# Chaining the second and third sums of a squared-relu group in PSUM, and adding every product into its output quadrants

## The chip, the cores and the metric

The kernel runs on one core of one Trainium2 chip. The metric is the device time of one execution in microseconds; the time shown is the median of several runs. All matrix products are float32r products made of three matmuls: each operand is cut into a high and a low part, and high x high, low x high and high x low are summed in PSUM.

## The reference

Two transformer-like blocks of width 1024 over 512 tokens. The first has two layers; each layer ends with a squared-relu MLP, and these two MLPs are what the change touches:

```python
def sq_relu_mlp(h, w_up, w_down):          # 1024 -> 4096 -> 1024
    return jnp.square(jax.nn.relu(h @ w_up)) @ w_down

# in first_block, for each of the two layers
h = rms_norm(x, ln_mlp_pre[i])
f = sq_relu_mlp(h, mlp_w_up[i], mlp_w_down[i])
x = x + rms_norm(f, ln_mlp_post[i]).astype(x.dtype)
```

The rest (a gated linear attention and a windowed attention before these MLPs, a second block with convolution, dilated attention and a gated MLP behind them) stays as it is.

## The kernel before, in words

The 4096 hidden columns of a layer are done in four parts of 1024. For the first three, the down projection is a seven-product (Strassen-like) scheme instead of eight products: a group "seven{layer}{o}" with o = 0 to 2, six groups in the kernel. The last part goes through the plain path (`t_ends`).

A group multiplies the hidden columns (AH, AL: high and low parts of seven combinations of the activations, made while the up products run) by seven combinations of four weight quadrants b11, b12, b21, b22. Each of the seven products ("b11", "b21", "t1", "b22", "t2", "t3", "t4") has two halves h = 0 and 1, so a group is 14 units. A unit is one weight tile of 128 x 1024 and 12 matmuls of 512 columns. The list STREAM gives their order: b11, b21, t1 (first halves), then their second halves, b22, t2, t3, t4. A product fills two PSUM banks (one per half of the 256 tokens that a combination has), by the table SEVEN_BANKS.

The weight tile of a unit comes into a raw slot (four of them, WR) by a DMA that SyncE issues. For t1 and t3, GpSimd then adds a second quadrant into the same slot with an accumulating DMA; for t2 and t4 it adds a further quadrant into the slot of t1, once the tile in it has been cut for t1 or t2. The order of GpSimd's issues is M_SUMS (`g_seven`). ScalarE makes the high part WH (`a_high`, L1299) and VectorE the low part WL (`v_low`, L2030), for which there are four slots; a slot is free when the unit four places earlier is done. Both engines run their programs in order: in step j of a group each first cuts unit j + 3 (`a_cut`, `v_cut`) and then does its other work. TensorE takes the units in order (`t_seven`): it waits for WL of the unit and, at the first half of a product, until the two banks are free.

VectorE empties the two banks of a product in one instruction of 128 x 1024 (`part`, L2448 in the first group of a layer, L2451 in the others), in the step after the product's second half: into four quadrants of MT and three buffers of PX, one accumulator for each product. Behind the third group, while the up products of the last part run, seven SBUF additions (`together`, L2460) make the four output quadrants from the seven accumulators. The last four weight tiles of the down projection may be cut when the seventh of these is done, since they lie over PX.

Of the kernel before, what the change touches and what calls it, by code (L numbers as in the profile page):

```python
# [144 lines left out]

def stream_of(name):

    return {"sevenf2": LAST_STREAM, "sevenv0": V_STREAM, "sevenw0": V_STREAM, "seveny0": Y_STREAM}.get(name, STREAM)


def plan(m, d):
# [70 lines left out]
    for layer in range(2):  # L222
        up, down = each(f"up{layer}", 32), each(f"down{layer}", 8)
        for o in range(3):
            add(f"up{layer}{o}", up[8 * o:8 * o + 8])
            seven(f"seven{layer}{o}", d[f"quart{layer}"][o].rearrange("j h p f -> h j p f"))
        add(f"up{layer}3", up[24:])
        add(f"down{layer}3", down, extra=m.EXTRA["mlp"], freed=("sum7", layer, 6))
        if layer == 0:
            add("swa_in", each("swa_in", 10))  # L230
            add("swa_out", each("swa_out", 8), extra=m.EXTRA["swa"], freed=("pv", "w", 15))
# [29 lines left out]
def memory(nc):  # L261
# [38 lines left out]
    def arena(name, shape, kb, dt=F32):  # L300
        return over(name, shape, base + int(kb * KB), dt)
# [13 lines left out]

    m.AH = arena("AH", [128, 4, 7, 256], 0, F32R)
    m.AL = arena("AL", [128, 4, 7, 256], 28, F32R)
    m.PX = arena("PX", [128, 3, 2, 512], 59)
    m.H3H = arena("H3H", [128, DC, T], 0, F32R)
    m.H3L = arena("H3L", [128, DC, T], 16, F32R)  # L320
    m.RW = over("RW", [128, 2, 2, T], acc)
# [61 lines left out]
def quarter(m, i, j):  # L383

    return m.MT[:, 2 * i:2 * i + 2, 512 * j:512 * j + 512]


def partial(m, what):

    if what in ("b21", "t2", "t3"):  # L390
        return m.PX[:, ("b21", "t2", "t3").index(what)]
    return quarter(m, *{"b11": (0, 0), "b22": (0, 1), "t4": (1, 0), "t1": (1, 1)}[what])


def mixes(m, key):
# [41 lines left out]
class Taps:  # L437
# [14 lines left out]
    def take(self, n):  # L452
# [22 lines left out]
GLA_O = (6, 7)  # L475
STREAM = [("b11", 0), ("b21", 0), ("t1", 0), ("b11", 1), ("b21", 1), ("t1", 1), ("b22", 0), ("b22", 1), ("t2", 0), ("t2", 1),
          ("t3", 0), ("t3", 1), ("t4", 0), ("t4", 1)]
LAST_HIDDEN = (7, 15, FC2 - 1)
LAST_STREAM = [("b11", 0), ("b21", 0), ("t1", 0), ("b22", 0), ("b11", 1), ("b21", 1), ("t1", 1), ("t2", 0), ("t2", 1), ("b22", 1),
               ("t3", 0), ("t3", 1), ("t4", 0), ("t4", 1)]  # L480
SIDE = {"b11": 0, "b21": 1, "t4": 2, "t3": 3, "t1": 4, "t2": 5, "b22": 6}
SIDE_PART = {0: "a", 1: "b", 2: "b", 3: "s", 4: "s", 5: "s", 6: "s"}
M_SUMS = [("t1", 0), ("t1", 1), ("t2", 0), ("t2", 1), ("t3", 0), ("t3", 1), ("t4", 0), ("t4", 1)]
F_SUMS = [("t1", 0), ("t1", 1), ("t2", 0), ("t3", 0), ("t3", 1), ("t2", 1), ("t4", 0), ("t4", 1)]
LAST_BANKS = {"b11": 0, "b21": 2, "t1": 4, "b22": 6, "t2": 0, "t3": 0, "t4": 2}
LAST_PARTS = {"b11": (((0, 0), 1),), "b21": (((0, 0), 1),), "t1": (((0, 1), 1), ((1, 1), 1)), "b22": (((0, 1), 1),),
# [9 lines left out]
Y_BANKS = {"b11": 4, "b21": 6, "t1": 2, "t2": 4, "b22": 2, "t3": 4, "t4": 0}  # L496
V_DECAYS, V_TURNS = (1, 4, 7, 10), (3, 6, 9, 12)
SEVEN_BANKS = {"b11": 0, "b21": 2, "t1": 4, "b22": 6, "t2": 0, "t3": 2, "t4": 4}
FFN_PARTS = {"b11": (((0, 0), 1), ("u2", 1)), "b21": (((0, 0), 1),), "t1": (((0, 1), 1), ((1, 1), 1)), "b22": (((0, 1), 1),),
             "t2": (("u2", 1),), "t3": (((1, 0), 1), ((1, 1), -1)), "t4": (((1, 0), 1),)}  # L500
GLA_DS = ((2, 3), (4, 5))
# [443 lines left out]
def t_seven(e, k, key, o):  # L945

    m, name = k.m, f"seven{key}{o}"
    u, stream = k.at[name], stream_of(name)
    last = name == "sevenf2"

    def pairs(j, h, b, f, v, start, stop):

        x = k.units[u + j]
        n = x.n // 4
        for q in range(n):
            p, w = 2 * h + q, slice(512 * q, 512 * q + 512)
            xh, xl = m.AH[:, p, f, tile(v)], m.AL[:, p, f, tile(v)]
            e.wait_ge(*k.on("side", key, 4 * o + p, SIDE_PART[f]))
            e.matmul(m.ps[b + v], xh, x.wh[:, w], start=start and q == 0, stop=False, skip_group_check=last)  # L959
            e.matmul(m.ps[b + v], xl, x.wh[:, w], start=False, stop=False, skip_group_check=last)  # L960
            y = e.matmul(m.ps[b + v], xh, x.wl[:, w], start=False, stop=stop and q == n - 1, skip_group_check=last)  # L961
        return y

    for j, (what, h) in enumerate(stream):
        b, f = (LAST_BANKS if last else SEVEN_BANKS)[what], SIDE[what]
        e.wait_ge(*k.on("wlo", u + j))
        if last and what == "t4":
            if h == 0:
                continue
            for v in range(2):  # L970
                e.wait_ge(*k.on(*k.free[b + v]))
                pairs(j - 1, 0, b, f, v, True, False)
                y = pairs(j, 1, b, f, v, False, True)
                y.then_inc(*(k.mark("unit", u + j) if v else k.mark("front", what)))
            continue
        for v in range(2):
            if h == 0:
                e.wait_ge(*k.on(*k.free[b + v]))
            y = pairs(j, h, b, f, v, h == 0 and not (last and what in ("t2", "t3")), h == 1)
            if last and what == "t2" and h and v == 0:  # L980
                y.then_inc(*k.mark("front", what))
        y.then_inc(*k.mark("unit", u + j))
        if h == 1:
            for v in range(2):
                k.free[b + v] = ("part", key, o, what, v) if last and what == "t2" else ("part", key, o, what)
# [1440 lines left out]
def v_mlp(e, k, layer):  # L2426
    m, at = k.m, k.at
    post, then = ("post_mlp0", "mix1") if layer == 0 else ("post_mlp1", "in2")

    def others(p):  # L2430

        v_mix(e, k, layer, p, ("sqr", at[f"up{layer}{p // 4}"] + 2 * (p % 4) + 1))
        v_side_b(e, k, layer, p)

    def plain(i):

        p, c = i // 2, i % 2
        e.wait_ge(*k.on("hidh", at[f"up{layer}3"] + i - 24))
        e.tensor_tensor(m.H3L[:, i - 24, :], m.RW[:, p % 2, c, :], m.H3H[:, i - 24, :].bitcast(F32), A.subtract).then_inc(
            *k.mark("hid", layer, i - 24))  # L2440

    def part(o, what):

        u = at[f"seven{layer}{o}"] + STREAM.index((what, 1))
        src, acc = pair(m, SEVEN_BANKS[what]).rearrange("p (a f) -> p a f", a=2), partial(m, what)
        e.wait_ge(*k.on("unit", u))
        if o == 0:
            e.tensor_copy(acc, src).then_inc(*k.mark("part", layer, o, what))  # L2448
        else:
            e.wait_ge(*k.on("part", layer, o - 1, what))  # L2450
            e.tensor_tensor(acc, src, acc, A.add).then_inc(*k.mark("part", layer, o, what))  # L2451

    def together(n):

        c11, c12, c21, c22 = (quarter(m, i, j) for i in range(2) for j in range(2))
        p2, u2, u3 = (m.PX[:, i] for i in range(3))
        out, a, b, op = ((u2, c11, u2, A.add), (c11, c11, p2, A.add), (u3, u2, u3, A.add), (c21, c21, u3, A.add),
                         (c12, c12, c22, A.add), (c12, c12, u2, A.subtract), (c22, c22, u3, A.subtract))[n]
        e.wait_ge(*(k.on("sum7", layer, n - 1) if n else k.on("part", layer, 2, "t4")))
        e.tensor_tensor(out, a, b, op).then_inc(*k.mark("sum7", layer, n))  # L2460

    def ups(o):

        u = at[f"up{layer}{o}"]
        for j in range(8):
            v_cut(e, k, u + j + 3)
            if o == 3:
                if j:
                    plain(24 + j - 1)
                    together(j - 1)  # L2470
                continue
            if j % 2:
                v_side_a(e, k, layer, 4 * o + j // 2)
            if j > 1 and j % 2 == 0:
                others(4 * o + j // 2 - 1)
            if j > 2 and j % 2:
                v_side_s(e, k, layer, 4 * o + j // 2 - 1)

    def seven(o):

        u = at[f"seven{layer}{o}"]
        for j in range(14):
            v_cut(e, k, u + j + 3)
            if j == 0:
                others(4 * o + 3)
            if j == 1:
                v_side_s(e, k, layer, 4 * o + 3)
            if j and STREAM[j - 1][1]:
                part(o, STREAM[j - 1][0])
        part(o, STREAM[13][0])  # L2490

    for o in range(3):
        ups(o)
        seven(o)
    ups(3)
    v_cut(e, k, at[f"down{layer}3"] + 3)
    plain(31)
    v_ends(e, k, at[f"down{layer}3"], at["swa_in" if layer == 0 else "glu"], post, then)
# [513 lines left out]
def g_seven(e, k, key, o):  # L3012

    m, name = k.m, f"seven{key}{o}"
    u = k.at[name]
    for what in F_SUMS if key == "f" else M_SUMS:
        j = stream_of(name).index(what)
        x = k.units[u + j]
        e.wait_ge(*k.on(*x.sum_of))
        e.dma_start(raw(m, x.raw)[:, 0:128 * x.n], x.more, accum_op=A.add).then_inc(*k.mark(f"added{x.raw}", u + j, by=16))  # L3020
# [243 lines left out]
```

## Time and profile before

| | |
|---|---|
| runs | 1903.17 us median of 3 (1901.72, 1903.17, 1905.87) |
| span of the profiled execution | 1900.5 us; it has no other time of its own, and is 2.7 us below the median |
| TensorE (PE) busy | 1890.5 us, 99% |
| VectorE (DVE) busy | 1339.4 us, 70% |
| ScalarE (ACT) busy | 985.3 us, 52% |
| GpSimd (POOL) busy | 95.3 us, 5% |
| matmuls of the groups (L959 to L961) | 3 x 490, of which 6 x 168 in the two MLPs |
| DMA | 249.8 MB, mean 131 GB/s |

Matmuls are pipelined: one of 512 columns is shown with 0.39 us, and the next begins 0.23 us after it. The six groups begin at 270.4, 352.0, 433.6, 757.6, 839.2 and 920.8 us. Units are counted from 0 within a group.

### The profile page before, as it was taken

The numbers are of one execution on the slowest core, as the hardware profiler recorded it, in microseconds if no ns is written. First come the engines' busy times: TensorE is split into PE (matmuls) and PEld (weight loads), VectorE is DVE, ScalarE is ACT, GpSimd is POOL, SyncE is SP. The second block draws the span as 40 slices with busy tenths as digits, with TensorE's granted clock in tenths as the row PEclk, the third lists the DMA queues.
The fourth block names the chain that finished last, engine by engine and source line by source line (L and its number), as shares of the span: only waits on it lengthen the run. The fifth ranks groups of instructions, "written<-read, shape, count | busy, mean of one in ns | idle before, by whom it ended". The sixth has DMA issues, their size and how long they took to land. (4 is left out here: it accounts for less than half of the span.)

```text
span 1900.5 us, 25399 instructions
## 1 busy us (share of the span) xinstructions
PE 1890.5 (99%) x9486; PEld 1555.8 (82%) x9486; DVE 1339.4 (70%) x1988; ACT 985.3 (52%) x1587; POOL 95.3 (5%) x114
## 2 busy tenths in 40 slices
PE   9999999999999999999999999999999999999999
PEld 8877888887888778888888988667788888888887
DVE  7656665656566766665566788998897867767867
ACT  5634464544546746454444435788445446545454
POOL 0100000101000000000100000000000000100101
PEclk9999999999999999999999999999999999999999
DMA  7632156757323114756752356222224634644735
GB/s 230 155 100 94 73 142 180 166 162 202 123 79 144 46 56 132 201 139 173 180 162 67 112 143 167 89 90 78 89 91 143 166 89 155 155 148 118 199 95 122
DMA packets 69676, 249.79 MB, mean 131 GB/s; under 512 B 7730, under 2 KB 7986, under 8 KB 68916
## 3 DMA queue, kind: packets, MB, share of 16 engines
q1 hardware_dynamic: 55728, 198.88, 31.0%
q0 software_dynamic: 13824, 49.29, 14.8%
q8 instruction: 77, 1.26, 0.3%
q14 instruction: 43, 0.35, 0.1%
q10 hardware_dynamic: 4, 0.00, 0.0%
HBM read 246.05 MB, written 2.10 MB: 131 GB/s over the span
## 5 line engine op out<-in xcount | busy, mean ns | idle before, releaser
L545 PE MATMUL ps<-HH,WH 128*128 128x512 f32 (+1 forms) x1696 | 626.2, 369 | 0.9 <-ACT AT L1736 0.9
L547 PE MATMUL ps<-HH,WL 128*128 128x512 f32 (+1 forms) x1696 | 621.2, 366 | 0.0
L546 PE MATMUL ps<-HL,WH 128*128 128x512 f32 (+1 forms) x1696 | 620.9, 366 | 0.0
L1299 ACT ACTIVATE WH<-WR 128x1024 fp32r<-128x1024 f32 x333 | 348.9, 1056 | 479.8 <-PE ps L547 315.3
L2030 DVE TENSOR_TENSOR WL<-WR,WH 128x1024 fp32r<-128x1024 f32 (+1 forms) x332 | 403.1, 1218 | 263.1 <-ACT WH L1299 262.4
L545 PEld LDWEIGHTS ps<-HH,WH 128*128 128x128 f32 x1696 | 319.9, 189 | 62.5 <-issue 11.6
L547 PEld LDWEIGHTS ps<-HH,WL 128*128 128x128 f32 x1696 | 319.9, 189 | 52.2
L546 PEld LDWEIGHTS ps<-HL,WH 128*128 128x128 f32 x1696 | 320.0, 189 | 50.7
L959 PE MATMUL ps<-WH,AH 128*128 128x512 f32 x490 | 191.0, 390 | 0.4 <-DVE WL L2030 0.4
L960 PE MATMUL ps<-WH,AL 128*128 128x512 f32 x490 | 190.7, 389 | 0.0
L961 PE MATMUL ps<-WL,AH 128*128 128x512 f32 x490 | 190.6, 389 | 0.0
L2576 DVE SCALAR_TENSOR_TENSOR M<-AP,PAR,M 128x512 f32<-128x512 f32 x240 | 166.1, 753 | 0.1
L959 PEld LDWEIGHTS ps<-WH,AH 128*128 128x128 f32 x490 | 92.0, 188 | 20.8 <-DVE WL L2030 1.7
L961 PEld LDWEIGHTS ps<-WL,AH 128*128 128x128 f32 x490 | 92.0, 188 | 19.0
L960 PEld LDWEIGHTS ps<-WH,AL 128*128 128x128 f32 x490 | 92.0, 188 | 19.0
L1919 ACT ACTIVATE UP<-ps 128x512 f32<-128x512 f32 x44 | 26.4, 599 | 116.5 <-PE ps L547 116.5
L3020 POOL DMA_DIRECT2D WR<-in_quart x48 | 41.8, 988 | 818.5 <-DMA WR<-in_quart 751.2
L2881 DVE SCALAR_TENSOR_TENSOR RW<-UP,PAR,RW 128x512 f32<-128x512 f32 x44 | 33.1, 752 | 43.3 <-ACT RW L1925 42.5
L2881 DVE SCALAR_TENSOR_TENSOR M<-UP,PAR,M 128x512 f32<-128x512 f32 x44 | 33.1, 752 | 37.7 <-ACT M L1925 36.9
L1307 ACT ACTIVATE HL<-X 128x1024 fp32r<-128x1024 f32 x24 | 25.4, 1060 | 34.8 <-DVE X L2091 24.4
L1318 ACT ACTIVATE HH<-ps 128x512 fp32r<-128x512 f32 x48 | 26.1, 594 | 31.2 <-PE ps L598 31.0
L1527 ACT ACTIVATE RW<-RW 128x512 f32<-128x512 f32 x64 | 40.6, 634 | 2.0
(386 smaller groups left out, 2606.9 us busy)
## 6 DMA issues: line engine op xcount, KB each, us to landing
WR<-in_up SPq DMA_DIRECT2D x96, 512.0 KB, 4.2
WR<-in_quart SPq DMA_DIRECT2D x60, 512.0 KB, 3.6
WR<-in_quart POOLq DMA_DIRECT2D x48, 512.0 KB, 6.3
WR<-in_in SPq DMA_DIRECT2D x48, 512.0 KB, 3.6
WR<-in_down SPq DMA_DIRECT2D x16, 512.0 KB, 3.5
WR<-in_quartf SPq DMA_DIRECT2D x14, 512.0 KB, 3.5
WR<-in_quartf POOLq DMA_DIRECT2D x14, 512.0 KB, 5.6
MT<-in_up SPq DMA_DIRECT2D x12, 512.0 KB, 4.1
```

Of the source, the lines that this page charges most:

```text
L545: e.matmul(ps, wh, hi[:, c, cols], start=c == 0, stop=False)
L546: e.matmul(ps, wh, lo[:, c, cols], start=False, stop=False)
L547: y = e.matmul(ps, wl, hi[:, c, cols], start=False, stop=c == x.n - 1)
L959: e.matmul(m.ps[b + v], xh, x.wh[:, w], start=start and q == 0, stop=False, skip_group_check=last)
L960: e.matmul(m.ps[b + v], xl, x.wh[:, w], start=False, stop=False, skip_group_check=last)
L961: y = e.matmul(m.ps[b + v], xh, x.wl[:, w], start=False, stop=stop and q == n - 1, skip_group_check=last)
L1299: e.activation(x.wh[:, 0:n], raw(m, x.raw)[:, 0:n], AF.Copy).then_inc(*k.mark("whi", u))
L1527: e.activation(buf, buf, AF.Square).then_inc(*k.mark("sqr", u))
L2030: e.tensor_tensor(x.wl[:, 0:n], raw(m, x.raw)[:, 0:n], x.wh[:, 0:n].bitcast(F32), A.subtract).then_inc(*k.mark("wlo", u))
L2576: e.scalar_tensor_tensor(m.M[:, c, :], m.AP[:, c, t:t + T], par(m, "conv_w", c * 31 + t, 1), m.M[:, c, :], A.mult, A.add).then_inc(*k.mark ...
L2881: e.scalar_tensor_tensor(tmp, m.UP[:, 2 * (i % 2) + g, t:t + T], par(m, "fcw", (i + FC2 * g) * 3 + t, 1), tmp, A.mult, A.add).then_inc(*k. ...
L3020: e.dma_start(raw(m, x.raw)[:, 0:128 * x.n], x.more, accum_op=A.add).then_inc(*k.mark(f"added{x.raw}", u + j, by=16))
```

## The change

The t2 products are accumulated onto b11 in banks 0 and 1, and t3 onto t2 in the same banks: their first matmuls no longer start a new accumulation. t4 goes ahead of t3, in TensorE's stream and in GpSimd's additions, and takes banks 2 and 3. So t2's banks hold b11 + t2 and t3's hold b11 + t2 + t3 when VectorE reads them, and every product is added to or subtracted from its output quadrants at once: nine operations in a group in place of seven, four of them copies in the first group of a layer. PX and `together` are gone. The last weight tiles of the down projection are free when the third group's last unit is done. The loops of `v_mlp` and `a_mlp` that place a cut and an evacuation in a step stay as they are, with M_STREAM for STREAM.

```diff
 def stream_of(name):
 
+    if name[:6] in ("seven0", "seven1"):
+        return M_STREAM
...
-        add(f"down{layer}3", down, extra=m.EXTRA["mlp"], freed=("sum7", layer, 6))
+        add(f"down{layer}3", down, extra=m.EXTRA["mlp"], freed=("unit", at[f"seven{layer}2"] + 13))
...
-    m.PX = arena("PX", [128, 3, 2, 512], 59)
...
+M_STREAM = STREAM[:10] + STREAM[12:] + STREAM[10:12]
...
-M_SUMS = [("t1", 0), ("t1", 1), ("t2", 0), ("t2", 1), ("t3", 0), ("t3", 1), ("t4", 0), ("t4", 1)]
+M_SUMS = [("t1", 0), ("t1", 1), ("t2", 0), ("t2", 1), ("t4", 0), ("t4", 1), ("t3", 0), ("t3", 1)]
...
+M_BANKS = {"b11": 0, "b21": 2, "t1": 4, "b22": 6, "t2": 0, "t3": 0, "t4": 2}
+M_STARTS = ("b11", "b21", "t1", "b22", "t4")
+M_PARTS = {"b11": (((0, 0), 1),), "b21": (((0, 0), 1),), "t1": (((0, 1), 1), ((1, 1), 1)), "b22": (((0, 1), 1),),
+           "t2": (((0, 1), -1),), "t4": (((1, 0), 1),), "t3": (((1, 1), -1), ((1, 0), 1))}
...
     for j, (what, h) in enumerate(stream):
-        b, f = (LAST_BANKS if last else SEVEN_BANKS)[what], SIDE[what]
+        b, f = (LAST_BANKS if last else M_BANKS if chained else SEVEN_BANKS)[what], SIDE[what]
...
-            y = pairs(j, h, b, f, v, h == 0 and not (last and what in ("t2", "t3")), h == 1)
+            y = pairs(j, h, b, f, v, h == 0 and not (last and what in ("t2", "t3")) and not (chained and what not in M_STARTS), h == 1)
...
     def part(o, what):
 
-        u = at[f"seven{layer}{o}"] + STREAM.index((what, 1))
-        src, acc = pair(m, SEVEN_BANKS[what]).rearrange("p (a f) -> p a f", a=2), partial(m, what)
+        u = at[f"seven{layer}{o}"] + M_STREAM.index((what, 1))
+        src = pair(m, M_BANKS[what]).rearrange("p (a f) -> p a f", a=2)
         e.wait_ge(*k.on("unit", u))
-        if o == 0:
-            e.tensor_copy(acc, src).then_inc(*k.mark("part", layer, o, what))
-        else:
-            e.wait_ge(*k.on("part", layer, o - 1, what))
-            e.tensor_tensor(acc, src, acc, A.add).then_inc(*k.mark("part", layer, o, what))
...
+        for to, sign in M_PARTS[what]:
+            acc = quarter(m, *to)
+            if to not in prior:
+                e.wait_ge(*k.on("turned", f"mlp{layer}", 3, 1))
+                if sign > 0:
+                    e.tensor_copy(acc, src).then_inc(*k.mark("part", layer, o, what, to))
+                else:
+                    e.tensor_scalar(acc, src, -1.0, None, A.mult).then_inc(*k.mark("part", layer, o, what, to))
+            else:
+                e.wait_ge(*k.on("part", *prior[to]))
+                if sign > 0:
+                    e.tensor_tensor(acc, src, acc, A.add).then_inc(*k.mark("part", layer, o, what, to))
+                else:
+                    e.tensor_tensor(acc, acc, src, A.subtract).then_inc(*k.mark("part", layer, o, what, to))
+            prior[to] = (layer, o, what, to)
+        k.also("part", layer, o, what)
...
                     plain(24 + j - 1)
-                    together(j - 1)
...
-            if j and STREAM[j - 1][1]:
-                part(o, STREAM[j - 1][0])
-        part(o, STREAM[13][0])
+            if j and M_STREAM[j - 1][1]:
+                part(o, M_STREAM[j - 1][0])
+        part(o, M_STREAM[13][0])
```

## Rows read from the trace of the kernel before

**Rows 1.** Page, busy time, share of the span and instructions of TensorE.

```profile
PE 1890.5 (99%) x9486; PEld 1555.8 (82%) x9486; DVE 1339.4 (70%) x1988; ACT 985.3 (52%) x1587; POOL 95.3 (5%) x114
```

**Rows 2.** Waits of TensorE: us in total, times, longest.

```profile
PE ps L959 <- DVE WL L2030: 0.4, 2, 0.2
```

**Rows 3.** Timeline of TensorE, six groups: start, us, [idle before]; units 0, 12, ...

```profile
270.36 0.39 PE L959 MATMUL ps<-WH,AH 128*128 128x512 f32 x1
303.00 0.39 PE L959 MATMUL ps<-WH,AH 128*128 128x512 f32 x1
...
384.60 0.39 PE L959 MATMUL ps<-WH,AH 128*128 128x512 f32 x1
...
467.09 0.39 PE L959 MATMUL ps<-WH,AH 128*128 128x512 f32 x1
...
470.16 0.50 PE L959 MATMUL ps<-WH,AH 128*128 128x512 f32 x1 [0.19 <-DVE WL L2030]
...
790.21 0.39 PE L959 MATMUL ps<-WH,AH 128*128 128x512 f32 x1
...
871.81 0.39 PE L959 MATMUL ps<-WH,AH 128*128 128x512 f32 x1
...
953.41 0.39 PE L959 MATMUL ps<-WH,AH 128*128 128x512 f32 x1
```

**Rows 4.** Timeline of ScalarE, first group: high cuts of units 10 and 13.

```profile
292.18 1.06 ACT L1299 ACTIVATE WH<-WR 128x1024 fp32r<-128x1024 f32 x1 [4.18 <-DMA WR<-in_quart]
...
301.51 2.96 ACT L1299 ACTIVATE WH<-WR 128x1024 fp32r<-128x1024 f32 x3 [2.54 <-DMA WR<-in_quart]
```

**Rows 5.** Timeline of VectorE, first group: cuts of units 5, 8, 9, 13, then t2.

```profile
277.27 1.22 DVE L2030 TENSOR_TENSOR WL<-WR,WH 128x1024 fp32r<-128x1024 f32 x1
...
285.31 1.23 DVE L2030 TENSOR_TENSOR WL<-WR,WH 128x1024 fp32r<-128x1024 f32 x1 [0.36 <-ACT WH L1299]
...
288.03 1.23 DVE L2030 TENSOR_TENSOR WL<-WR,WH 128x1024 fp32r<-128x1024 f32 x1 [0.36 <-ACT WH L1299]
...
302.61 1.23 DVE L2030 TENSOR_TENSOR WL<-WR,WH 128x1024 fp32r<-128x1024 f32 x1 [2.37 <-ACT WH L1299]
303.75 1.22 DVE L2448 COPY PX<-ps 128x1024 f32<-128x1024 f32 x1
```

**Rows 6.** Instructions of line 2460: count, ns min/median/max, first and last start.

```profile
L2460 DVE TENSOR_TENSOR MT<-MT,PX x8: 1217/1219/1221, 487.7 to 1000.7; 128x1024 f32<-128x1024 f32 x8
```

**Rows 7.** Timeline of VectorE, evacuation of t2 in groups two to six.

```profile
384.01 1.22 DVE L2451 TENSOR_TENSOR PX<-ps,PX 128x1024 f32<-128x1024 f32 x1
...
470.02 1.22 DVE L2451 TENSOR_TENSOR PX<-ps,PX 128x1024 f32<-128x1024 f32 x1
...
790.80 1.22 DVE L2448 COPY PX<-ps 128x1024 f32<-128x1024 f32 x1
...
871.53 1.22 DVE L2451 TENSOR_TENSOR PX<-ps,PX 128x1024 f32<-128x1024 f32 x1
...
955.63 1.22 DVE L2451 TENSOR_TENSOR PX<-ps,PX 128x1024 f32<-128x1024 f32 x1
```

**Rows 8.** Timeline of GpSimd, first group: additions of t2's second half, t3, t4.

```profile
278.78 0.86 POOL L3020 DMA_DIRECT2D WR<-in_quart  x1 [10.12 <-DVE WL L2030]
286.29 0.86 POOL L3020 DMA_DIRECT2D WR<-in_quart  x1 [6.64 <-DMA WR<-in_quart]
288.60 2.65 POOL L3020 DMA_DIRECT2D WR<-in_quart  x3 [1.45 <-DMA WR<-in_quart]
```

**Rows 9.** DMA queues from 286 to 302 us: packets, MB, share of 16 engines.

```profile
q0 software_dynamic: 576, 2.10, 72.3%
q1 hardware_dynamic: 410, 1.49, 24.2%
```

**Rows 10.** Windows, first 4 us: busy time of each engine, granted clock, DMA.

```profile
0.00:4.00 4.00, 2.07 (x4) 1.17 (x4) 0.28 (x2) 1.49 (x2) 0.20 (x4) 1.00 0.55 163
```

More of the change, by code:

```diff
@@ L385, in quarter @@
     return m.MT[:, 2 * i:2 * i + 2, 512 * j:512 * j + 512]
[L388 to L392, printed above, removed]
 def mixes(m, key):
@@ L482 @@
 SIDE_PART = {0: "a", 1: "b", 2: "b", 3: "s", 4: "s", 5: "s", 6: "s"}
-M_SUMS = [("t1", 0), ("t1", 1), ("t2", 0), ("t2", 1), ("t3", 0), ("t3", 1), ("t4", 0), ("t4", 1)]
+M_SUMS = [("t1", 0), ("t1", 1), ("t2", 0), ("t2", 1), ("t4", 0), ("t4", 1), ("t3", 0), ("t3", 1)]
+V_SUMS = [("t1", 0), ("t1", 1), ("t2", 0), ("t2", 1), ("t3", 0), ("t3", 1), ("t4", 0), ("t4", 1)]
 F_SUMS = [("t1", 0), ("t1", 1), ("t2", 0), ("t3", 0), ("t3", 1), ("t2", 1), ("t4", 0), ("t4", 1)]
@@ L948, in t_seven @@
     u, stream = k.at[name], stream_of(name)
-    last = name == "sevenf2"
+    last, chained = name == "sevenf2", key in (0, 1)
     def pairs(j, h, b, f, v, start, stop):
@@ L958, in pairs @@
             e.wait_ge(*k.on("side", key, 4 * o + p, SIDE_PART[f]))
-            e.matmul(m.ps[b + v], xh, x.wh[:, w], start=start and q == 0, stop=False, skip_group_check=last)
-            e.matmul(m.ps[b + v], xl, x.wh[:, w], start=False, stop=False, skip_group_check=last)
-            y = e.matmul(m.ps[b + v], xh, x.wl[:, w], start=False, stop=stop and q == n - 1, skip_group_check=last)
+            e.matmul(m.ps[b + v], xh, x.wh[:, w], start=start and q == 0, stop=False, skip_group_check=last or chained)
+            e.matmul(m.ps[b + v], xl, x.wh[:, w], start=False, stop=False, skip_group_check=last or chained)
+            y = e.matmul(m.ps[b + v], xh, x.wl[:, w], start=False, stop=stop and q == n - 1, skip_group_check=last or chained)
         return y
     for j, (what, h) in enumerate(stream):
-        b, f = (LAST_BANKS if last else SEVEN_BANKS)[what], SIDE[what]
+        b, f = (LAST_BANKS if last else M_BANKS if chained else SEVEN_BANKS)[what], SIDE[what]
         e.wait_ge(*k.on("wlo", u + j))
@@ L2428, in v_mlp @@
     post, then = ("post_mlp0", "mix1") if layer == 0 else ("post_mlp1", "in2")
+    prior = {}
     def others(p):
@@ L2442, in part @@
     def part(o, what):
-        u = at[f"seven{layer}{o}"] + STREAM.index((what, 1))
-        src, acc = pair(m, SEVEN_BANKS[what]).rearrange("p (a f) -> p a f", a=2), partial(m, what)
+        u = at[f"seven{layer}{o}"] + M_STREAM.index((what, 1))
+        src = pair(m, M_BANKS[what]).rearrange("p (a f) -> p a f", a=2)
         e.wait_ge(*k.on("unit", u))
-        if o == 0:
-            e.tensor_copy(acc, src).then_inc(*k.mark("part", layer, o, what))
-        else:
-            e.wait_ge(*k.on("part", layer, o - 1, what))
-            e.tensor_tensor(acc, src, acc, A.add).then_inc(*k.mark("part", layer, o, what))
[L2453 to L2460, printed above, removed]
+        for to, sign in M_PARTS[what]:
[14 more added lines that the diff above has]
+        k.also("part", layer, o, what)
     def ups(o):
@@ L3015, in g_seven @@
     u = k.at[name]
-    for what in F_SUMS if key == "f" else M_SUMS:
+    for what in F_SUMS if key == "f" else M_SUMS if key in (0, 1) else V_SUMS:
         j = stream_of(name).index(what)
```

## The prediction

> **What bounds the kernel now.** I read the page's busy shares first, then the list of what TensorE waited for, then the timelines of TensorE, VectorE, ScalarE and GpSimd inside one squared-relu group, and last the same few instants in the other five groups. The reader is to see in the first that TensorE is busy for 1890.5 of 1900.5 us [rows 1], and in the second that the matmuls of the groups (line 959) waited 0.4 us in all, for cut weights [rows 2]. So nothing that only frees another engine can give much back, and everything that makes TensorE wait is paid in full.
>
> A group is 14 units. In the first one the unit 0 starts at 270.36 and unit 12 at 303.00 [rows 3], so a unit lasts 32.64 / 12 = 2.72 us. In these 2.72 us ScalarE and VectorE must cut one raw weight tile into its high part (WH) and low part (WL), three units ahead. The last raw tiles of a group are made by accumulating DMAs from GpSimd, and these are late: ScalarE starts the high cut of unit 10 at 292.18 and that of unit 13 at 301.51, each released by such a DMA [rows 4], and VectorE's low cut of unit 13 starts at 302.61 [rows 5], 2.9 us before TensorE needs it at 305.72 (303.00 + 2.72). The supply of weights keeps up, with little in hand. That margin is what the change touches.
>
> **The change, part by part.**
>
> *The removed additions.* Seven SBUF additions per layer in the stage behind the third group go, 14 in all at 1.22 us [rows 6]: 17.1 us of VectorE. Each group gets two more PSUM operations of VectorE (nine for seven): 6 x 2 x 1.22 = 14.6 us. VectorE is the same within 2.5 us. In the stage of the removed additions TensorE runs eight up products behind one another and is busy as everywhere [rows 1], so I cost their removal at 0: the up products hide it. For the same reason the earlier release of the last weight tiles (unit 13 in place of the seventh addition), the copies that become subtractions of the same shape and the new wait for the turned rows (satisfied before the first group) are 0. The second operation on t1 runs to about 291.6 (288.03 + 3 x 1.2), before ScalarE has begun the high cut of unit 10 at 292.18 [rows 4, 5]. The two on t3 stand at the end of the group; bank 0 and 1 are next wanted by the third up product behind it, two products of 24 matmuls later, and are free long before.
>
> *The chained products: a new wait.* t2 is accumulated onto b11 in banks 0 and 1, t3 onto t2 in the same banks. TensorE may not begin t3 (now unit 12) before VectorE has read t2 out. Before, t3 had banks 2 and 3, free since b21, and nothing waited for t2's evacuation until the up products. The place of that evacuation in VectorE's program does not move: the loop at j = 10 first cuts unit 13 and only then evacuates t2. In the first group t2's last matmul is over at about 297.6 (unit 10's start), but VectorE copies it out only at 303.75, right behind the low cut of unit 13 at 302.61 [rows 5], which waits for the high cut at 301.51, which waits for the group's last accumulating DMA [rows 4]. So in the changed kernel unit 12 waits for a DMA that feeds unit 13. Nothing circular stands in it: that DMA needs the low cuts of units 7 and 9 alone.
>
> The price in each group, if all else stays in place: start of t2's evacuation + 1.22 us + 0.05 us to hand over, less the start of unit 12 [rows 3, 5, 7]. First: 303.75 + 1.27 - 303.00 = 2.02. Second: 384.01 + 1.27 - 384.60 = 0.68. Third: 470.02 + 1.27 - 467.09 = 4.20, less the 0.35 that unit 12 there lost afterwards before unit 13 (470.16 - 467.09 - 2.72) and that is then covered: 3.85. Fourth: 790.80 + 1.27 - 790.21 = 1.86. Fifth: 871.53 + 1.27 - 871.81 = 0.99. Sixth: 955.63 + 1.27 - 953.41 = 3.49. Sum 12.9 us. The third and sixth are worst because the row-gain load sits in SyncE's queue ahead of t3's raw tiles.
>
> *t4 ahead of t3.* GpSimd now issues the additions as t1, t1, t2, t2, t4, t4, t3, t3. t4's first one needs the low cut of unit 8, t4's second that of unit 9. GpSimd issues 0.29 us after such a cut (277.27 + 1.22, then 278.78) [rows 5, 8]. So the four last additions, issued before at 286.29, 288.60, 289.5 and 290.4 (the last three in one block of 2.65 us [rows 8]), go out at 285.31 + 1.51 = 286.8, 288.03 + 1.51 = 289.5, 290.4 and 291.3. The first is 0.5 us later and the last 0.9 us. The software queue takes 72.3% of the 16 DMA engines over 16 us, the hardware queue 24.2% [rows 9]: the engines are full, an addition costs 0.723 x 16 / 4 = 2.9 us of them, and the four land one behind the other. So the last landing moves with the first issue: 0.5 us later, in the four groups in which t3's raw tiles are in time. In the third and sixth they held up the first addition before and no longer do, so I take no shift. That adds 4 x 0.5 = 2.0 us. Bounds: the four land back to back at the least, from 286.82 plus the lead of the first one before (292.18 - 286.29 - 2.9 = 3.0) plus 11.6, at 301.4 in place of the 302.0 that I take, so 0.6 us less for each group; at the most each lands as slowly as the last one may (a quarter more than 2.9, about 3.6 us), which is 2 us more.
>
> *After the wait* the weight load is not hidden: the first matmul behind a wait lasts 0.50 us, the others 0.39 [rows 3], 0.1 us x 6 = 0.6. Bounds 0 and 0.2 each.
>
> Sum: 12.9 + 2.0 + 0.6 = 15.5 us on the profiled span of 1900.5, 1916.0. The median of the runs shown stands 2.7 us above that span; with the same distance 1918.7. The six waits are of 1 to 4 us and nothing behind them can make them good, since TensorE is the engine that has no reserve.
>
> **Clock.** The granted clock is 1.00 of the higher level (2.4 GHz) even in the first 4 us, where TensorE was busy for 2.07 us only [rows 10]. Waits of up to 4 us in the middle of full work are in no row. The Trainium skill, "TensorE: Matmul & The Clock Gate", section "A second HAM failure mode: psum-queue depth-cycling", says that small idle gaps between groups of matmuls, from cycling through PSUM banks, make the clock swing between its two levels and cost throughput. By that rule each of the six waits would be followed by matmuls at 1.2 GHz. It speaks against the change; no row of this trace shows it, so it is a rival and not a term.
>
> **Rivals.**
> - *The additions come early enough and the wait is hidden* (the other side: not slower). If the last accumulating DMA lands 2.5 us (first group) to 4 us (sixth) earlier than I take it, t2 is out before unit 12 is due. For it: t4's additions no longer queue behind t3's raw tiles. Against: issue times move later, not earlier, in four groups, and the engines are full [rows 9]. It decides at a landing of about 299.5 in the first group. Then only the waits of the third group go (0.4 us [rows 2], with the weight reloads behind them under 1 us): 1902.
> - *The freed vector work counts.* 17.1 us of additions leave the stage behind the third groups. Against: 14.6 us come back in the groups and TensorE waited for none. At best half of the 10 us in which TensorE is not busy [rows 1]: 1898.
> - *The chain does not bind* (the change does not do what it says: TensorE has t2's evacuation ahead of the cut after all). By the order of the loop this is nearly excluded: 1903.
> - *The clock falls behind each wait.* At half the level a unit of 2.72 us takes 5.44; one or two units at that level behind each wait give 16 to 33 us more: 1935 to 1951.
>
> **How the numbers follow.** Forecast 0.79, with its own range from the bounds: 11 us (0.6 less in six groups, no reload cost) to 28 us (2 us more in six groups), 1914 to 1931, most of it below 1926. Early additions 0.11, freed vector work 0.03, no binding 0.02, clock 0.05. A measurement tells about 0.2%, 3.8 us, from no change. Faster 0.03; same 0.13 (early additions and no binding); slower 0.84. The range leaves the same-time cases out below with a part of the smallest waits, and the clock case above: 1907 to 1927.
>
> **What would show it.** In the profile after: line 959's wait for VectorE's evacuation (a line of the new `part`) at some 13 to 17 us in six times, where [rows 2] have 0.4 for the cuts; each at unit 12, none at unit 10; the low cut of unit 13 directly ahead of t2's subtraction on VectorE; units of 2.72 us before and behind. Wrong would be: no such wait (early additions: t2's subtraction then starts before unit 11 is over), waits at units 10 or 11 (t4's cuts late instead), a granted clock below 1.00 in the groups, or a gain in the stage behind the third groups.

## The result, and the profile after

The changed kernel took 1935.49 us (median of 4 runs, 1932.61 to 1937.72) and the kernel before 1903.68 us beside it: a ratio of 1.0167, interval 1.0155 to 1.0179. That is 31.8 us slower, twice the 15.5 us of the sum and outside the range. The profiled execution has a span of 1933.1 us, 32.6 above the one before. Three readings account for it.

**TensorE waits, and also works longer.** First the page's busy line of the changed kernel, to be held against [rows 1], then what ended TensorE's waits, against [rows 2] (us in total, times, longest).

```profile
PE 1901.2 (98%) x9486; PEld 1563.0 (81%) x9486; DVE 1338.3 (69%) x1986; ACT 984.9 (51%) x1587; POOL 95.1 (5%) x114
```

```profile
PE ps L959 <- issue: 22.0, 6, 5.3
```

The same number of matmuls is busy for 10.7 us more (1901.2 against 1890.5), and six waits of 22.0 us in all have come. The view gives their releaser as "issue", that is nothing it could name; the other engines show whom they wait for. The timeline of TensorE has them at the first matmul of unit 12 in each group (start, duration, idle before):

```profile
306.95 0.47 PE L959 MATMUL ps<-WH,AH 128*128 128x512 f32 x1 [3.18 <-issue]
...
392.00 0.77 PE L959 MATMUL ps<-WH,AH 128*128 128x512 f32 x1 [3.21 <-issue]
...
482.18 0.76 PE L959 MATMUL ps<-WH,AH 128*128 128x512 f32 x1 [5.32 <-issue]
...
810.59 0.52 PE L959 MATMUL ps<-WH,AH 128*128 128x512 f32 x1 [3.77 <-issue]
...
896.44 0.76 PE L959 MATMUL ps<-WH,AH 128*128 128x512 f32 x1 [2.39 <-issue]
...
983.94 0.47 PE L959 MATMUL ps<-WH,AH 128*128 128x512 f32 x1 [4.13 <-issue]
```

Counted from the start of unit 11 (300.89 in the first group), less a unit's 2.72 us, the six come to 3.34, 3.37, 5.63, 3.93, 2.56 and 4.30, 23.1 us in all.

**What they wait for.** ScalarE's high cuts of units 10 to 13 in the first group, VectorE's work behind the last two, and the additions that GpSimd issued for these units:

```profile
293.31 1.06 ACT L1299 ACTIVATE WH<-WR 128x1024 fp32r<-128x1024 f32 x1 [4.70 <-DMA WR<-in_quart]
295.79 1.06 ACT L1299 ACTIVATE WH<-WR 128x1024 fp32r<-128x1024 f32 x1 [1.42 <-DMA WR<-in_quart]
299.75 1.06 ACT L1299 ACTIVATE WH<-WR 128x1024 fp32r<-128x1024 f32 x1 [2.89 <-DMA WR<-in_quart]
303.40 2.95 ACT L1299 ACTIVATE WH<-WR 128x1024 fp32r<-128x1024 f32 x3 [2.59 <-DMA WR<-in_quart]
```

```profile
300.84 1.22 DVE L2030 TENSOR_TENSOR WL<-WR,WH 128x1024 fp32r<-128x1024 f32 x1 [1.59 <-ACT WH L1299]
304.49 1.23 DVE L2030 TENSOR_TENSOR WL<-WR,WH 128x1024 fp32r<-128x1024 f32 x1 [2.42 <-ACT WH L1299]
305.63 1.22 DVE L2461 TENSOR_TENSOR MT<-MT,ps 128x1024 f32<-128x1024 f32 x1
```

```profile
287.44 0.86 POOL L3022 DMA_DIRECT2D WR<-in_quart  x1 [7.19 <-DVE WL L2030]
290.16 2.65 POOL L3022 DMA_DIRECT2D WR<-in_quart  x3 [1.85 <-DVE WL L2030]
```

This is the chain of the prediction, link by link: the last accumulating DMA has landed when ScalarE starts the high cut at 303.40, the high cut lasts until 304.46, the low cut of unit 13 starts at 304.49, t2's subtraction (line 2461) at 305.63, and unit 12 at 306.95, 0.10 us after its end at 306.85. VectorE stood idle for 2.42 us ahead of the cut with t2 ready in PSUM all that time: unit 10 began at 298.17.

**The clock falls behind five of the six waits.** Windows over unit 12 in each group, and one in the second group just after unit 13 (us, busy time with the number of instructions of PE, PEld, DVE, ACT and POOL, then the granted clock, DMA share, GB/s):

```profile
306.90:309.70 2.80, 2.75 (x12) 2.35 (x13) 2.80 (x3) 0.00 (x0) 0.00 (x0) 1.00 0.81 215
392.00:397.20 5.20, 5.20 (x12) 4.15 (x13) 3.30 (x3) 0.00 (x0) 0.00 (x0) 0.50 0.83 287
482.10:487.00 4.90, 4.82 (x12) 3.83 (x13) 3.38 (x3) 0.00 (x0) 0.00 (x0) 0.54 0.77 244
810.60:815.00 4.40, 4.40 (x12) 3.50 (x13) 3.30 (x3) 0.00 (x0) 0.00 (x0) 0.61 0.85 269
896.40:900.70 4.30, 4.26 (x12) 3.44 (x13) 3.34 (x3) 0.00 (x0) 0.00 (x0) 0.63 0.83 259
983.90:988.30 4.40, 4.36 (x12) 3.46 (x13) 3.34 (x3) 0.00 (x0) 0.00 (x0) 0.62 0.81 252
397.40:400.20 2.80, 2.80 (x13) 2.28 (x12) 1.23 (x1) 1.06 (x1) 0.00 (x0) 0.92 0.00 1
```

A granted clock of 0.50 is the level of 1.2 GHz for the whole window; 0.54 to 0.63 is a mean over both levels. In the second group the matmuls of unit 12 last 0.63 us and start 0.43 us apart, where 0.39 and 0.23 are usual. From its first matmul to that of unit 13, unit 12 takes 2.80, 5.26, 4.89, 4.41, 4.31 and 4.38 us; over 2.72 that is 9.7 us in all, which is most of the additional busy time. Waits and slow units make 32.8 us, and the span grew by 32.6. The match is closer than the terms allow: the kernel before lost 1.2 us in its third group itself (470.16 less 433.6, less 13 units [rows 3]), and 0.6 us of the growth stands ahead of the first group.

### The profile page after: what moved, and what is told of

Its sections match the earlier page's. It is cut to its first block, busy times and chain, and to the rows that moved or that the text cites. A ratio compares the mean times of both kernels' runs of the same rounds, so it can differ in the third digit from the quotient of the medians.

```text
span 1933.1 us, 25411 instructions
## 1 busy us (share of the span) xinstructions
PE 1901.2 (98%) x9486; PEld 1563.0 (81%) x9486; DVE 1338.3 (69%) x1986; ACT 984.9 (51%) x1587; POOL 95.1 (5%) x114
## 3 DMA queue, kind: packets, MB, share of 16 engines
q8 instruction: 78, 1.28, 0.3%
## 4 chain that ended last, share of the span: by engine, by line
PE 89%; DMA 5%; DVE 3%; ACT 1%; issue 1%; POOL 0%; DVEq 0%; ACTq 0%
PE ps L545 19%; PE ps L547 19%; PE ps L546 18%; DMA WR<-in_quart 5%; PE ps L959 3%; PE ps L961 3%; PE ps L960 3%; PE ps L574 3%; PE ps L576 3%; PE ps L575 3%; PE ps L715 1%; PE ps L717 1%; PE ps L716 1%; DVE WL L2030 1%; PE ps L598 1%
## 5 line engine op out<-in xcount | busy, mean ns | idle before, releaser
L545 PEld LDWEIGHTS ps<-HH,WH 128*128 128x128 f32 x1696 | 319.8, 189 | 62.1 <-issue 11.6
L959 PE MATMUL ps<-WH,AH 128*128 128x512 f32 x490 | 195.4, 399 | 22.0 <-issue 22.0
```

The costliest lines, as they stand in the source:

```text
L545: e.matmul(ps, wh, hi[:, c, cols], start=c == 0, stop=False)
```

## The experiments

The theory behind the first runs (theory A below): the loss is the wait of unit 12 for t2's evacuation, which stands behind the cut of unit 13, and the clock that falls in these waits. The rivals: the moved products and additions alone cost it (rival B: t4 ahead of t3), or something else in the new evacuation does (rival C below: its instructions, their place, the freed buffers), and the chain is only where it shows.

**t2 read out ahead of the cut of unit 13.** All else stays as changed.

```diff
+            if j == 10:
+                part(o, "t2")
...
-            if j and M_STREAM[j - 1][1]:
+            if j and j != 10 and M_STREAM[j - 1][1]:
```

> The changed kernel with one line moved: at step 10 VectorE evacuates t2 before it cuts unit 13, not behind it. Theory A (the wait): the whole loss is TensorE's wait at unit 12 for an evacuation that stands behind a cut that waits for the last accumulating DMA, and the lower clock behind that wait. Then t2 is out about 1.3 us after unit 9 ends, 4 us before unit 12 is due; no wait, clock 1.00: 1900 to 1904 us, a little under the kernel before (no waits in the third group). Rival B (the order): t4 ahead of t3 makes the cuts themselves late, so waits of 1 us or more stay at units 10 to 13: 1908 to 1920. Rival C (the chain): adding onto banks that are being read, or nine evacuations in a group, slow the group by themselves: above 1907 with matmuls longer than 0.39 us or units longer than 2.72 us without waits.

1906.43 against 1904.24 us, ratio 1.0013 (1.0003 to 1.0023), PE busy 1892.2. VectorE in the first group, with the subtraction now in what had been idle time ahead of the cut, then TensorE's waits and its first matmul of unit 12 in the sixth group:

```profile
300.06 1.23 DVE L2030 TENSOR_TENSOR WL<-WR,WH 128x1024 fp32r<-128x1024 f32 x1 [1.54 <-ACT WH L1299]
301.20 1.21 DVE L2461 TENSOR_TENSOR MT<-MT,ps 128x1024 f32<-128x1024 f32 x1
303.71 3.50 DVE L2030 TENSOR_TENSOR WL<-WR,WH 128x1024 fp32r<-128x1024 f32 x3 [1.30 <-ACT WH L1299]
```

```profile
PE ps L959 <- issue: 4.5, 3, 2.6
PE ps L959 <- DVE WL L2030: 0.9, 1, 0.9
```

```profile
958.34 0.47 PE L959 MATMUL ps<-WH,AH 128*128 128x512 f32 x1 [2.64 <-issue]
```

So 29 of the 31.8 us hang on the order of two VectorE instructions. The time is still 2.4 us above the 1904 that was expected at most. What is left is in the third and sixth groups (waits of 1.73 and 2.64 us at unit 12, in the third 0.9 at unit 13 too) and, by 0.17 us, in the fourth. Behind the wait of 2.64 us the clock fell (unit 12 took 4.42 us), behind the one of 1.73 it did not.

**Only the order of the products.** The kernel before, with t4 ahead of t3 in TensorE's stream and in GpSimd's additions; banks, accumulators and the seven additions at the end stay.

```diff
+M_STREAM = STREAM[:10] + STREAM[12:] + STREAM[10:12]
...
-M_SUMS = [..., ("t3", 0), ("t3", 1), ("t4", 0), ("t4", 1)]
+M_SUMS = [..., ("t4", 0), ("t4", 1), ("t3", 0), ("t3", 1)]
```

> The kernel before with only t4 put ahead of t3 (TensorE's stream and GpSimd's additions); own banks, own accumulators and the seven SBUF additions stay. Theory A: nothing waits for t2's evacuation, so 1901 to 1905, no wait over 0.7 us in any group. Rival B: the order alone makes the last additions late and units 10 to 13 wait: 1908 to 1920. Rival C expects 1903 too.

1904.34 against 1904.24, ratio 1.0002 (0.9993 to 1.0011). The later additions cost only the last cuts' waits, 1.4 us in three times. By itself the order has no cost that can be measured, and this rival falls. It does bring the last additions down later, which the account of the prediction comes back to.

**The wait filled with matmuls that nobody uses.** Twelve matmuls of 512 columns on a free bank stand ahead of unit 12's wait for its banks (and behind that for its cut weights), so that TensorE idles less and all else is late by as much as before.

```diff
+        if chained and what == "t3" and h == 0:
+            e.wait_ge(*k.on(*k.free[6]))
+            for _ in range(12):
+                e.matmul(m.ps[6], m.AH[:, 0, 0, tile(0)], k.units[u + j].wh[:, 0:512], start=True, stop=True, ...)
```

> The changed kernel with twelve matmuls of 512 columns on a free bank (2.7 us at full clock) put ahead of unit 12's wait; they compute nothing that is used. If the 10.7 us by which TensorE's busy time grew are the lower clock that follows the gap, the waits end when they did (t2's evacuation does not move), TensorE's gap shrinks to 0 to 3 us, the clock stays at 1.00 in most groups and the time falls by 6 to 10 us, to 1925 to 1930, although 72 matmuls were added. If the clock falls for another reason, the time stays at 1935 or rises to 1936.

1925.55 against 1904.24, ratio 1.0108 (1.0092 to 1.0123). The first matmul of unit 12 in the first group, the waits (this time with their releaser: line 2466 is t2's subtraction), and windows from unit 12's start in the first group and from within the filler in the second:

```profile
306.48 0.50 PE L959 MATMUL ps<-WH,AH 128*128 128x512 f32 x1 [0.63 <-DVE MT L2466]
```

```profile
PE ps L959 <- DVE MT L2466: 5.9, 6, 1.8
```

```profile
306.40:309.40 3.00, 2.92 (x13) 2.42 (x14) 3.00 (x4) 0.00 (x0) 0.00 (x0) 1.00 0.63 193
388.00:391.00 3.00, 3.00 (x14) 2.24 (x12) 2.16 (x2) 2.71 (x3) 0.00 (x0) 1.00 0.47 176
```

Twelve matmuls at 0.227 us in six groups are 16.3 us, and 5.9 of waiting for the evacuation are left. Counted from unit 11 to unit 12, as above, unit 12 is 25.1 us late in all, 2.0 more than in the changed kernel (23.1). But the granted clock stays at 1.00 in the whole run, unit 12 takes 17.2 us over the six groups in place of 26.0, and the kernel is 9.9 us faster with 72 more matmuls in it. That separates the two terms: 9 to 10 us are the clock's, and the rest is lateness, whether TensorE idles in it or not.

**The loads of the up products held back.** SyncE begins to load a part's up tiles only when unit 13 of the group ahead has been cut.

```diff
+    for layer in range(2):
+        for o in range(3):
+            if u == k.at[f"up{layer}{o + 1}"]:
+                e.wait_ge(*k.on("wlo", k.at[f"seven{layer}{o}"] + 13))
```

> The changed kernel, but SyncE issues the loads of the up tiles behind a group only when unit 13 of the group is cut. Theory: the last two additions land 3.7 to 4.6 us apart in place of 2.9 because the up loads share the DMA engines; without them the last landing comes 1.5 to 2 us earlier in each group, the six waits fall from 23 us to 11 to 14, fewer clock falls: 1915 to 1926. Rival: the last addition lands some 11 us after its issue whatever the loads do: 1933 to 1937. If the late loads make the up products wait, that shows as waits at line 545.

1922.17 against 1904.24, ratio 1.0096 (1.0082 to 1.011). The waits are 15.6 us for 22.0 (16.6 counted from unit to unit: 2.20, 1.79, 3.74, 2.72, 1.13, 4.99), and PE busy is 1894.8. ScalarE's high cuts of units 10 to 13 in the first group:

```profile
292.89 1.06 ACT L1299 ACTIVATE WH<-WR 128x1024 fp32r<-128x1024 f32 x1 [4.62 <-DMA WR<-in_quart]
295.44 1.06 ACT L1299 ACTIVATE WH<-WR 128x1024 fp32r<-128x1024 f32 x1 [1.49 <-DMA WR<-in_quart]
299.40 1.06 ACT L1299 ACTIVATE WH<-WR 128x1024 fp32r<-128x1024 f32 x1 [2.90 <-DMA WR<-in_quart]
301.93 1.06 ACT L1299 ACTIVATE WH<-WR 128x1024 fp32r<-128x1024 f32 x1 [1.47 <-DMA WR<-in_quart]
```

The last addition lands 2.53 us behind the third, in place of 3.65 (15.7 us over the six groups, in place of 23.7): that part of the lateness is the up loads on the same DMA engines. The third lands 3.96 us behind the second in both kernels (23.1 us over the six groups, and 20.4), so that spacing is not theirs. The sixth group went against the expectation: its wait grew from 4.30 to 4.99. The clock fell only there and in the third group, behind waits of 4.83 and 3.58 us; behind 2.04, 1.63, 2.56 and 0.97 us it stayed at 1.00. Windows over unit 12 in the third and sixth groups:

```profile
474.45:478.60 4.15, 4.15 (x12) 3.28 (x13) 0.67 (x1) 1.57 (x2) 0.00 (x0) 0.65 0.93 367
970.77:975.10 4.33, 4.33 (x12) 3.48 (x13) 0.86 (x1) 1.70 (x2) 0.00 (x0) 0.62 0.93 352
```

**The chain with the old order of products.** t3 comes ahead of t4 again, as unit 10, and is still accumulated onto t2; in a second kernel t2 is also read out ahead of the cut of unit 13.

```diff
-M_STREAM = STREAM[:10] + STREAM[12:] + STREAM[10:12]
+M_STREAM = STREAM
...
-M_SUMS = [..., ("t4", 0), ("t4", 1), ("t3", 0), ("t3", 1)]
+M_SUMS = [..., ("t3", 0), ("t3", 1), ("t4", 0), ("t4", 1)]
```

> The changed kernel with t3 back ahead of t4, in TensorE's stream and in GpSimd's additions; the chain in banks 0 and 1 and the place of every cut and evacuation stay. Theory A: t3 is now unit 10 and still waits for t2's evacuation behind the cut of unit 13. That evacuation ends as in the kernel before or a little later (305 us in the first group), unit 10 is due at 297.6: waits of 7.5, 6.1, 9, 7.3, 6.4 and 8.9 us, 45 us in all, with the low clock behind each some 10 to 12 us more: 1950 to 1965. If t4 ahead of t3 were what costs (rival B): 1903 to 1912.

> The same, with t2's evacuation moved ahead of the cut of unit 13 at step 10. Theory A: it then stands behind the cut of unit 12 (301.5 in the first group with the evacuation) where unit 10 is due at 297.6, so about 4 us of wait stay in each group, 20 to 26 in all, with 8 to 11 us for the clock: 1930 to 1942. If moving the evacuation were enough by itself: 1903 to 1908.

1961.65 us, ratio 1.031 (1.029 to 1.0329), and 1943.79 us, ratio 1.0201 (1.0184 to 1.0218), both against 1904.20. The waits of the first and of the second:

```profile
PE ps L959 <- issue: 45.1, 6, 9.0
...
PE ps L959 <- issue: 29.6, 6, 7.3
```

With two units less between t2 and t3 the same chain costs 57 us, and putting t4 between them takes 26 of these away. The second kernel waited 29.6 us, above the 20 to 26 expected, and its time is above the range expected too. Here the order of VectorE's program alone doesn't help enough, since the cuts of unit 12 ahead of the evacuation are late too (that low cut starts at 299.09 in the first group, where unit 10 was due at 297.05).

**t3 in banks of its own.** t3 starts afresh in banks 4 and 5; the third sum then lacks b11 and t2. VectorE's program stays as changed.

```diff
-M_BANKS = {..., "t2": 0, "t3": 0, "t4": 2}
-M_STARTS = ("b11", "b21", "t1", "b22", "t4")
+M_BANKS = {..., "t2": 0, "t3": 4, "t4": 2}
+M_STARTS = ("b11", "b21", "t1", "b22", "t4", "t3")
```

> The changed kernel with t3 begun afresh in banks 4 and 5 (free since t1 was read): it leaves out b11 + t2 from the third sum. VectorE's program is that of the changed kernel, t2's evacuation behind the cut of unit 13 with it. Theory A: only the wait for the bank goes, so the six waits go: 1902 to 1906, with at most the small waits for cuts in the third and sixth groups (1 to 4 us). Rival C (nine evacuations, or the place of the evacuation by itself, cost): above 1910.

1903.20 against 1904.20, ratio 0.9999 (0.9989 to 1.0008). VectorE in the first group, and TensorE's waits at line 959:

```profile
303.99 1.23 DVE L2030 TENSOR_TENSOR WL<-WR,WH 128x1024 fp32r<-128x1024 f32 x1 [2.25 <-ACT WH L1299]
305.13 1.21 DVE L2461 TENSOR_TENSOR MT<-MT,ps 128x1024 f32<-128x1024 f32 x1
```

```profile
PE ps L959 <- DVE WL L2030: 1.5, 3, 1.1
```

The subtraction is as late as in the changed kernel, and nobody waits for it: the waits shown are for cut weights. So it isn't the evacuation, its place or its nine operations that cost anything measurable, but only that unit 12 wants its banks.

**What holds up the third and sixth groups.** These have the row-gain load among their weight loads. One kernel adds to the earlier evacuation a gain load behind t3's raw tiles; one reads t2 out a step earlier still, ahead of the cut of unit 12 (j == 9); one does both.

```diff
-    fetch(e, k, at["seven02"] + 8)
+    fetch(e, k, at["seven02"] + 13)
```

> The first experiment (t2's evacuation ahead of the cut of unit 13) with the row-gain load behind t3's raw tiles and nothing else. If the gain load made the 5.4 us of waits that stayed there, they fall to the 1 to 2 us that the last experiment had: 1903 to 1905. If they stayed because the evacuation stands behind unit 12's cut, waits of 2 us or more at unit 12 of the third and sixth groups remain: 1905 to 1907.

> The other half: t2's evacuation ahead of the cut of unit 12, the gain load where it was. If the gain load is what makes t4's second and t3's additions late, unit 12 or 13 of the third and sixth groups still waits 1 to 3 us each for its own cut weights (line 959 on the low cut): 1904 to 1906. If the place of the evacuation was all, under 1 us of waits: 1902 to 1904.

> The changed kernel with t2's evacuation ahead of the cut of unit 12 (step 9), and with the row-gain load of the third and sixth groups issued behind t3's raw tiles in place of ahead of them. In the first experiment 5.4 us of waits stayed, all but 0.2 in these two groups: there the gain load makes t2's addition late, the cut of unit 9 with it, and t4's second addition and t3's additions queue behind that cut on GpSimd. Theory A with this: no wait of a group's matmul is left (under 0.5 us), clock 1.00: 1901 to 1904, level with the kernel before or up to 1.5 us under it. If the gain load is not the cause, waits of 2 to 5 us stay in the two groups: 1904 to 1907.

Gain load moved: 1903.39 against 1903.27, ratio 1.0001 (0.9992 to 1.001), waits 1.7 us where the first experiment had 5.4. Evacuation a step earlier, gain load where it was: 1903.82 against 1903.27, 1.0000 (0.9991 to 1.001), waits 2.7 us, none of them for the evacuation. Both: 1904.21 against 1904.20, 0.9999 (0.999 to 1.0008), waits 1.9 us, where under 0.5 was expected. By the waits, the gain load is behind two thirds of what the first experiment left over, and the place of the evacuation behind half; the two overlap. By the times, none of the three can be told from the kernel before, and hardly from the first experiment (1.0003 to 1.0023).

**A version to beat both.** The evacuation a step earlier, with the gain loads behind the eighth up tile of the last part; and, for comparison, the kernel before with the gain loads alone moved so.

```diff
-    fetch(e, k, at["seven02"] + 8)
+    fetch(e, k, at["up03"] + 7)
```

> t2's evacuation ahead of the cut of unit 12, and the gain load behind all up tiles of the last part, out of the way of the groups' additions (in the last run it sat between t3's raw tiles and t4's first addition, which landed 9 us after its issue). Expected: no waits in the third and sixth groups, under 0.7 us in the others; 1901 to 1904, not to be told from the kernel before (TensorE is busy for 1890 us in both). Slower than 1905 would mean a cost of the chained form besides the wait.

> The kernel before, unchanged but for the row-gain load behind all up tiles of the last part. The last run (chained form, evacuation first, gain load last) came to 0.9989 of the kernel before. If that 2 us is the gain load's, this run has it too: ratio 0.998 to 0.9995 and no waits of line 959. If it is the chained form's (fewer additions, other order): ratio 0.9995 to 1.001.

1901.33 against 1903.27, ratio 0.9989 (0.998 to 0.9997), with no wait at line 959, where the same kernel with the gain load in its old place waited 2.7 us; and 1902.04 against 1903.53, ratio 0.9991 (0.9981 to 1.0), with no such wait in the six groups. The first is the fastest version, 0.1% under the kernel before. The second gives about as much without the chain, so this gain is the gain load's and not shown to be the chained form's. Without its wait, the chained form cannot be told from the kernel before.

## Why the prediction was right or wrong

**The mechanism of the wait and its place held.** Six waits, each at unit 12 and none at unit 10, with t2's subtraction directly behind the cut of unit 13, as the prediction put it. The first experiment and the one with banks of its own show it from both sides: take away what makes unit 12 wait, and 29 us or all of the loss go. One reading of the prediction was off without consequence: the low cut of unit 13 started 3.1 us ahead of TensorE's need (305.72 less 302.61 [rows 5]), not 2.9.

**The edits costed at nothing cost nothing.** With t3 in banks of its own all of them are in place (nine operations, no `together`, the earlier release, the new order), and the ratio is 0.9999. VectorE's busy time fell by 1.1 us, within the 2.5 said. The freed vector work gave no gain that can be measured, and the rival in which the additions come early enough falls with the landings, which are later in every group. The weight load behind the wait was 0.6 us of the sum; where the clock stayed up, the first matmul took 0.47 us for 0.39, so this was of the right size and too small to matter.

**The step of the last landing failed.** "So the last landing moves with the first issue: 0.5 us later, in the four groups" was 2.0 us of the sum, and nothing in the third and sixth. The issue times came as worked out: against the start of the group, the first addition is issued 0.54 us later and the block of three 0.95 us later (287.44 and 290.16 less 270.97, against 286.29 and 288.60 less 270.36 [rows 3, 8]). But the last landing is 1.28 us later (303.40 less 270.97, against 301.51 less 270.36 [rows 3, 4]), more than either, and behind the block it took 13.2 us where it had taken 12.9. Over the six groups t2's evacuation starts later by 1.3, 2.6, 0.6, 2.0, 1.5 and 0.8 us, 8.8 in all for the 2.0 taken. The waits are 23.1 us for 14.9.

The new order of the additions does this by itself. In the kernel before with only that order changed, the last landing is later by 1.2, 1.9, 0.3, 1.5, 2.1 and 0.8 us, 7.9 in all. By the starts of ScalarE's cuts, nearly all of the 8.8 us stand in two places: the third of the four landings came 15.4 us behind the second over the six groups and now comes 20.4 behind it, and the last came 20.0 us behind the third and now comes 23.7. The first spacing goes with the order: 15.4 to 15.8 us in the four kernels with t3's additions ahead of t4's, 18.7 to 25.0 in the ten with t4's ahead. What makes it so is not shown; the up loads do not, since it was 23.1 with them held back. The second spacing is 15.7 with the up loads held back, but the kernel before had these loads too, so why they cost more here is not shown. With them held back, the first five groups wait 11.6 us (18.8 with them), where the prediction, with its 0.5 us, has 11.4; that is luck in part, since the first spacing is then still longer than before the change and the second shorter, and single groups are off by up to 0.6. The bounds ("2 us more" for a group) held the sum, the value taken did not.

That the third and sixth groups got no shift was also wrong: t4's second addition is issued at 465.78 in the third, 21.95 us after the group's start at 443.83, where the first group has 19.19. It waits for the cut of unit 9, whose high part ScalarE starts only at 463.17, after 4.42 us without work, when t2's second addition has landed; the gain load among the weight loads is behind that: with it moved, the same addition is issued 19.19 us after the start there too. ScalarE and GpSimd in the third group:

```profile
463.17 1.06 ACT L1299 ACTIVATE WH<-WR 128x1024 fp32r<-128x1024 f32 x1 [4.42 <-DMA WR<-in_quart]
...
465.78 2.65 POOL L3022 DMA_DIRECT2D WR<-in_quart  x3 [4.62 <-DVE WL L2030]
```

The third group also had its unit 12 priced too late: it is now due 32.7 us after the group's start (473.83 and 2.72, less 443.83), where the prediction took 33.5 from the kernel before (467.09 less 433.6 [rows 3]). That is 0.8 us more of wait.

**The step of the clock failed.** This is the larger term, 9.7 us, and the prediction's own sign of being wrong, a granted clock below 1.00 in the groups, came. The clock stood as a rival with a chance of 0.05 and a cost of 0 in the sum, since the row at hand was a granted clock of 1.00 in the kernel's first 4 us [rows 10]. That row was no evidence on what happens behind a wait in the middle of full work: there five of six waits were followed by 0.50 to 0.63. The Trainium skill, "TensorE: Matmul & The Clock Gate", section "A second HAM failure mode: psum-queue depth-cycling", says that frequent idle gaps between groups of matmuls make the clock swing between its two levels and cost throughput. This trace agrees that gaps cost throughput in this way, with 9.7 us of longer units, but here the gaps are single ones, each some 85 us or more after the one before. The filled wait gives 9.9 us back. As a rival it was priced at 16 to 33 us, for one or two units at the lower level behind each wait. Measured were 0.08, 2.54, 2.17, 1.69, 1.59 and 1.66 us, so less than one unit each. With the clock at that size and the waits as predicted, the sum would have been 25 us (14.9 + 9.7 + little), and the rest of the miss is the wait, which was mis-sized with the landing.

**What stays open.** Why the clock stayed up behind one of the six waits isn't settled. The length of a wait doesn't decide it alone: behind 3.18 us in the first group it held, behind 2.39 us in the fifth it fell. Nor is it shown why the third addition lands later behind the second when t4's additions go first, or why the up loads cost the last one more there.

## What to carry to other kernels

When a product is accumulated onto one that must be read out in between, put its reading ahead of every instruction in that engine's program that waits for something later than the product itself needs; with two units of another product between the two, the loss fell that way from 1.7% to 0.1%, and with the reading a step earlier still to nothing that can be measured; with no unit between them it fell only from 3.1% to 2.0%. Price a new wait in a TensorE that has no reserve twice, for its length and for the units behind it at the lower clock, unless a row of the same kind of stretch shows that the clock holds. When issues move on full DMA engines, ask for the last landing which transfers share the engines until then, not only when the first is issued, and don't carry the spacing of the landings over to another order.

## What the runs had to show of the hardware

A single wait of 2.4 to 5.3 us between stretches of unbroken matmuls was followed in five cases of six by a granted clock between 0.50 and 0.63 over the next unit, and in the second group, the deepest fall, by 0.92 again behind unit 13. In the other runs, waits of 0.97 to 2.56 us with the up loads held back and one of 1.73 us with the earlier evacuation left it at 1.00, and one of 2.64 us did not. Behind all twelve waits of 3.8 to 9.0 us in the two kernels with the old order it fell, and the unit behind took 4.4 to 5.3 us for 2.72. Twelve unused matmuls in the wait made the whole kernel 9.9 us faster than the same kernel with TensorE idle there.

Three accumulating DMAs of 512 KB that were issued back to back, behind an earlier one still under way, landed 2.5, 4.0 and 3.7 us one behind the other by the starts of ScalarE's cuts, the last one 13.2 us after the block began to be issued. With the up loads off the same DMA engines, the last came 2.53 us behind the one before it, in place of 3.65.
